# Second layer of a hybrid decoder trunk: the state-space mixer's operands turned at the layer boundary instead of in slots 2 to 4

## What is computed

```python
bb_re = f_re[..., None] * br - f_im[..., None] * bi
bb_im = f_re[..., None] * bi + f_im[..., None] * br
x_re = jnp.einsum('bsgi,gpi->bsgp', ug, bb_re)
x_im = jnp.einsum('bsgi,gpi->bsgp', ug, bb_im)
...                                   # h_t = a h_(t-1) + x_t, complex
y = (jnp.einsum('gip,bsgp->bsgi', c_re, h_re)
     - jnp.einsum('gip,bsgp->bsgi', c_im, h_im) + d_skip * ug)
```

## Time and profile before

| | |
|---|---|
| median of 3 runs | 969.76 us (968.94 to 971.78) |
| the profiled execution | 969.32 us, its span 967.6 us |
| PE busy | 937.2 us, 97% of the span |
| PEld busy | 785.7 us, 81% |
| DVE, ACT, POOL busy | 700.1, 591.8, 282.9 us |
| mean granted TensorE clock | 0.996 |
| DMA | 157.32 MB, 163 GB/s on average |

### The profile page before, as it was taken

How to read it: one execution, slowest core, us unless ns; L and a number is a source line. 1 busy time by engine, 2 the same in 40 slices (tenths; PEclk the granted TensorE clock), 3 DMA queues, 4 the chain that set the end, 5 groups by cost and what they waited for, 6 DMA issues and landing times. The chain is left out here.

```text
span 967.6 us, 16077 instructions
## 1 busy us (share of the span) xinstructions
PE 937.2 (97%) x5895; PEld 785.7 (81%) x5895; DVE 700.1 (72%) x1127; ACT 591.8 (61%) x955; POOL 282.9 (29%) x226
## 2 busy tenths in 40 slices
PE   8989999999999999999999999999999999999996
PEld 7879777777878888888889987777777788888885
DVE  6878967664666888798865668766557668777776
ACT  7426776768355765666654567767664566666654
POOL 0243334341420568466000224443206001011010
PEclk9989999999999999999999999999999999999999
DMA  7963433453554756556469543434535346655551
GB/s 215 269 195 106 134 129 131 131 159 103 174 174 137 199 189 201 175 194 195 135 164 272 153 131 112 135 118 117 174 131 174 131 152 199 213 174 195 194 175 44
DMA packets 138023, 157.32 MB, mean 163 GB/s; under 512 B 16641, under 2 KB 105321, under 8 KB 137962
## 3 DMA queue, kind: packets, MB, share of 16 engines
q1 hardware_dynamic: 137960, 156.51, 52.2%
q10 hardware_dynamic: 2, 0.00, 0.0%
HBM read 154.40 MB, written 1.05 MB: 161 GB/s over the span
## 5 line engine op out<-in xcount | busy, mean ns | idle before, releaser
L1672 DVE TENSOR_TENSOR wl<-ring,wh 128x1024 fp32r<-128x1024 f32 (+1 forms) x276 | 359.8, 1306 | 100.1 <-ACT wh L1357 98.9
L1357 ACT ACTIVATE wh<-ring 128x1024 fp32r<-128x1024 f32 (+1 forms) x276 | 287.9, 1045 | 153.1 <-PE pj L791 120.5
L791 PE MATMUL pj<-h,wh 128*128 128x512 f32 (+1 forms) x1344 | 297.0, 344 | 11.9 <-DVE wl L1672 10.0
L791 PE MATMUL pj<-wh,h 128*128 128x512 f32 (+1 forms) x832 | 273.4, 395 | 4.7 <-ACT gate L1344 2.4
L791 PEld LDWEIGHTS pj<-h,wh 128*128 128x128 f32 x1344 | 229.3, 192 | 39.9 <-issue 11.7
L791 PEld LDWEIGHTS pj<-wh,h 128*128 128x128 f32 x832 | 154.7, 188 | 47.4 <-issue 10.4
L791 PE MATMUL pj<-h,wl 128*128 128x256 f32 x1024 | 189.7, 284 | 0.0
L791 PEld LDWEIGHTS pj<-h,wl 128*128 128x128 f32 x1024 | 158.4, 192 | 6.9
L791 PE MATMUL pj<-wl,h 128*128 128x512 f32 (+1 forms) x416 | 159.5, 383 | 0.0
L2322 POOL TENSOR_TENSOR work<-work 128x512 f32<-128x512 f32 x20 | 40.8, 2040 | 266.7 <-DVE work L2120 199.7
L791 PEld LDWEIGHTS pj<-wl,h 128*128 128x128 f32 x416 | 78.4, 188 | 12.8
(11 more groups left out here) (304 smaller groups left out, 1241.5 us busy)
## 6 DMA issues: line engine op xcount, KB each, us to landing
ring<-in_ffn_w_up SPq DMA_DIRECT2D x44, 1024.0 KB, 5.1
ring<-in_w_in SPq DMA_DIRECT2D x40, 1024.0 KB, 5.1
ring<-in_ffn_w_down SPq DMA_DIRECT2D x22, 1024.0 KB, 4.9
ring<-in_w_in SPq DMA_DIRECT2D x16, 512.0 KB, 5.5
ring<-in_w_branch SPq DMA_DIRECT2D x8, 1024.0 KB, 5.1
ring<-in_w_out SPq DMA_DIRECT2D x8, 1024.0 KB, 5.1
ring<-in_w_branch SPq DMA_DIRECT2D x8, 512.0 KB, 6.0
ring<-in_w_in SPq DMA_DIRECT2D x8, 256.0 KB, 3.9
```

The costliest lines, as they stand in the source:

```text
L791: return nc.tensor.matmul(o, a, b, start=start, stop=stop, skip_group_check=True)
L1357: A(dst, src, ACT.Copy).then_inc(w_hi.sem, 1)
L1672: TT(dst, src, hi.bitcast(F32), ALU.subtract).then_inc(w_lo.sem, 1)
```

## The change

In the second layer alone (`l == 1`) the S5 operands are turned at the layer boundary; the first layer stays as it was.

- `s5_c` (eight turns) stands where the `idle(6, bO)` at the end of the first layer's MLP was. It uses `bO` and `bY` and first waits for `unit_out[1]` too. The last layer keeps its idle products.
- `s5_b(0)` (eight turns, into `bO` and `bY`) stands behind the turning of token tile 0, in place of the `idle(4)` there.
- `s5_direct` (64 instructions, into `bX[0]`) and `s5_b(1)` (eight turns) stand behind the turning of token tile 1, in place of the `idle(4)` there.
- ACT copies the turned operands out (`operands_out`, two copies each time) behind the split of piece 0, behind the squares of token tile 1 and behind the split of piece 4.
- DVE's `s5_diagonal` stands behind the split of piece 4.
- POOL's `s5_carried` keeps its place in POOL's queue, and waits in addition for `hq_done`, since it writes where the first compression weights lie.

```diff
             for l in range(DEPTH):
                 turn_normed(2 * l, 0)
+                if l:
+                    s5_b(l, 0, (bO, bY))
                 if l == 0:
                     pe.wait_ge(step_row.sem, 2)
                     nc.tensor.transpose(bO[:, 0:P], stP, ident).then_inc(lam_turned.sem, 1)
                     idle(4)
                     turn_normed(2 * l, 1)
-                idle(4)
+                    idle(4)
...
                 if l:
                     turn_normed(2 * l, 1)
-                    idle(4)
+                    s5_direct(l, bX[0])
+                    s5_b(l, 1, (bO, bY))
...
-                    if q == S5_C:
-                        s5_c()
-                    if q in S5_B:
-                        s5_b(S5_B.index(q))
-                    if q == S5_B[0]:
-                        s5_direct()
+                    if l == 0 and q == S5_C:
+                        s5_c(l, (bY, bX[0]))
+                    if l == 0 and q in S5_B:
+                        s5_b(l, S5_B.index(q), bX)
+                    if l == 0 and q == S5_B[0]:
+                        s5_direct(l, bY)
...
-                idle(6, bO)
+                if l + 1 < DEPTH:
+                    pe.wait_ge(unit_out[1].sem, unit_out[1].at(l, n // 2 + 1))
+                    s5_c(l + 1, (bO, bY))
+                else:
+                    idle(6, bO)
                 pe.wait_ge(a_split.sem, a_split.at(l, STEPS))
...
+            def operands_out(l, step, banks):
+
+                for h in range(2):
+                    n = 2 * step + h
+                    a.wait_ge(bc_turned.sem, bc_turned.at(l, n + 1))
+                    dst = (CL[:, 0], CL[:, 1], BL[:, 0:4], BL[:, 4:8], BL_im[:, 0:4], BL_im[:, 4:8])[n]
+                    A(dst, banks[h].rearrange("p (j q) -> p j q", j=JC), ACT.Copy).then_inc(bc_ready.sem, bc_ready.up())
...
                 if l:
                     split_hi(l, 0)
+                    operands_out(l, 0, (bO, bY))
                 square(n, 0, 0)
...
                 square(n, 1, 1)
+                if l:
+                    operands_out(l, 1, (bO, bY))
                 root(n, 1)
...
                 split_hi(l, 4)
+                if l:
+                    operands_out(l, 2, (bO, bY))
...
-                    if q in (S5_C, *S5_B):
-                        n = 2 * (q - S5_C)
-                        for n in (n, n + 1):
-                            a.wait_ge(bc_turned.sem, bc_turned.at(l, n + 1))
...
+                    if l == 0 and q in (S5_C, *S5_B):
+                        operands_out(l, q - S5_C, (bY, bX[0]) if q == S5_C else bX)
...
                 for s in range(3, 5):
                     split_lo(l, s)
+                if l:
+                    s5_diagonal(l, bX[0])
...
-                    if q == S5_B[1]:
-                        s5_diagonal()
+                    if l == 0 and q == S5_B[1]:
+                        s5_diagonal(l, bY)
...
                 def s5_carried():
 
+                    g.wait_ge(hq_done.sem, hq_done.at(l, 1))
                     g.wait_ge(bc_ready.sem, bc_ready.at(l, 2))
```

More of the change, by code:

```diff
@@ L865, in idle, with s5_c, s5_b, s5_direct @@
                     mm(o[:, 0:P], ident, ident, True, True)
+            def s5_c(l, banks):
+                for c in range(2):
+                    pe.wait_ge(cx_ready.sem, cx_ready.at(l, c + 1))
+                    for j in range(JC):
+                        ins = nc.tensor.transpose(banks[c][:, P * j:P * j + P], cx[:, c, j, :], ident)
+                    ins.then_inc(bc_turned.sem, bc_turned.up())
+            def s5_b(l, c, banks):
+                if c == 0:
+                    pe.wait_ge(bx_ready.sem, bx_ready.at(l, 2))
+                pe.wait_ge(bc_ready.sem, bc_ready.at(l, 2 + 2 * c))
+                for h in range(2):
+                    for j in range(4):
+                        s = 8 * h + 2 * j
+                        ins = nc.tensor.transpose(banks[h][:, P * j:P * j + P],
+                                                  bx[:, c, s:s + 2].rearrange("p t n i -> p (t n i)"), ident)
+                    ins.then_inc(bc_turned.sem, bc_turned.up())
+            def s5_direct(l, o):
+                pe.wait_ge(bc_ready.sem, bc_ready.at(l, 2))
+                for j in range(JC):
+                    for c in range(2):
+                        for e in range(4):
+                            r = 32 * e
+                            ins = nc.tensor.matmul(o[r:r + 32, P * j:P * j + P], bx[:, c, 4 * j + e, 0, :],
+                                                   CL[:, c, j, :], start=c == 0, stop=c == 1, skip_group_check=True,
+                                                   tile_position=(0, r))
+                ins.then_inc(k_done.sem, k_done.up())
             pe.wait_ge(ones_set.sem, 1)
@@ L1012, in cmp_turn @@
                     ins.then_inc(pc_done.sem, pc_done.up())
[L1014 to L1043, removed]
                 def nsa_scores(m):
@@ L1785, in turns, with s5_diagonal @@
                 v.wait_ge(turns_ready.sem, 1)
+            def s5_diagonal(l, o):
+                v.wait_ge(k_done.sem, k_done.at(l, 1))
+                at = [P, JC, 4, 32]
+                TT(K0.rearrange("p j (e i) -> p j e i", e=4), o.rearrange("p (j e i) -> p j e i", j=JC, e=4),
+                   kon[:, K_QUAD:K_QUAD + 4].rearrange("p (j e i) -> p j e i", j=1, i=1).broadcast_to(at), ALU.mult)\
+                    .then_inc(k_ready.sem, k_ready.up())
             def table(tmp, lo, hi, first, last):
@@ L2005, in s5_scan @@
                     ins.then_inc(g5_ready.sem, g5_ready.up())
[L2007 to L2013, removed]
                 if l:
```

## The result

| | before | after |
|---|---|---|
| median of 6 runs each, us | 970.07 (968.7 to 971.78) | 964.98 (963.45 to 966.09) |
| ratio | | 0.9947, 95% interval 0.9935 to 0.996 |
| profiled execution: time, span, us | 969.32, 967.6 | 965.8, 964.1 |

What follows compares the result with a forecast made beforehand. TensorE was taken to bound the kernel, in slots 1 to 5 but for one gap. -4.54 - 1.3 - 0.45 + 1.95 + 0.3 = -4.04 gave 965.3 from the profiled execution, 965.7 by the median; forecast 965.5, range 964.0 to 967.6.

Steps and rivals of the forecast that it cites:

- blocks out of slots 2 to 4, and the gap: Second layer: S5 blocks leaving slots 2 to 4, gain 4.54 us; split wait at slot 6 gone, gain 1.3.
- first layer's end: Ahead of the last down-projection: eight turns replace twelve idle instructions, gain 0.45 us, bounds 0 and 0.67.
- down-projection and tile 0: Token tile 0, TensorE: eight turns replace eight idle instructions, 1.03 against 1.06 us; nothing.
- tile 1: Token tile 1, TensorE: `s5_direct` and `s5_b(1)` replace idle products, 2.95 for 1.00, delaying `vg`; loss 1.95 us, bounds 1.7 and 2.2.
- ACT ahead of the `vg` copy-out: Behind piece 4's split: two ACT copies delay the `vg` copy-out and first `narrow`; loss 0.3 us, bounds 0 and 0.5.
- behind slot 6: From slot 6 on: the same work, 4 us earlier.
- Rival 4: Slots: weight supply sets their pace, the 5.8 us return as split waits; 971.1 us, chance 0.05.
- rival 2: Slot 6: the split wait stays or returns one or two slots on; gain 2.7 us, chance 0.12.
- Tile 0, ACT: ACT copies behind the squares, 1.08 us, fit its 1.24 wait ahead of the root; nothing, up to 0.2 without that cover.
- POOL: `s5_carried` starts about 10 us earlier; slowing a DVE split would meet 6.8 us of DVE waiting; nothing.
- Rival 5: Layer boundary: turning lets the clock fall, 2.7 us per fall; 973.3 us with three falls, chance 0.05.
- case 2: The outcome in which the gap at slot 6 stays or moves: 966.6 to 967.0 us, chance 0.12.

Runs made afterwards that it cites:

- e7: The changed kernel again, without an edit; 966.1 us, ratio 0.9966.
- e1: Changed kernel with `s5_direct`, the imaginary part, its copies and mask back in slots 3 and 4, idle products back at tile 1; 968.01 us.
- e2: Kernel before, with ACT's exponential of the compressed softmax ahead of the two `BL_im` copies in slot 4, both layers; 969.3 us.
- e5: Changed kernel plus four idle products (eight instructions) behind the turning of the imaginary part, ahead of `vg` of tile 1; 966.07 us.
- e9: Changed kernel with `s5_direct` in two halves (first at tile 0) and, in the first layer, DVE's slot 6 split ahead of the softmax; 962.23 us, ratio 0.9926.
- e8: Changed kernel, `s5_direct` halved (first at tile 0); first layer: ACT's exponential ahead of `BL_im` copies, DVE's slot 6 split ahead of softmax; 963.12 us, ratio 0.9934.
- e6: Changed kernel with the first half of `s5_direct` moved between the first and second `vg` groups of tile 0; 963.19 us.
- e3: Changed kernel with 56 more turns ahead of `s5_c` at the first layer's end; 973.01 us.

## Why the prediction was right, step by step

Predicted was 965.5 (964.0 to 967.6), measured 964.98 at first and 966.1 the second time (e7). The mechanism was right at each step, and the sizes by the marks are:

| step | predicted, us | measured, us | from |
|---|---|---|---|
| blocks out of slots 2 to 4, and the gap | -5.84 | -5.97 | N to S6, 68.04 to 62.07 |
| of it `s5_c` and `s5_b(0)` | | -1.86 | e1 |
| first layer's end | -0.45 | -0.51 | 0.85 in place of 1.36 |
| down-projection and tile 0 | 0 | -0.03 | 7.04 (483.79 to 490.83) against 7.07; from there to the second half of tile 1's turns 5.45 in both |
| tile 1 | +1.95 | +1.83 | 2.74 and 0.09 of switching, less 1.00 |
| ACT ahead of the `vg` copy-out | +0.3 | +0.02 | V to N |
| behind slot 6 | 0 | +0.13 | S6 to end |
| sum | -4.04 | -4.53 | |

**Slots and gap.** Both terms came as counted, and e1 and e2 separate them: the first two blocks alone give their length and leave the gap, ACT's order alone gives the gap and leaves the blocks. Rival 4, that weight supply sets the pace there, falls with e1. The gap didn't move either (rival 2). The timeline of ACT shows that the softmax had more room than I gave it:

```profile
558.79 1.28 ACT L1570 ACT_TABLE_LOAD   x1
560.73 0.41 ACT L1570 ACTIVATE cE<-work 128x240 f32<-128x240 f32 x1 [0.66 <-DVE work L1965]
```

And that of DVE:

```profile
560.29 0.41 DVE L1965 TENSOR_TENSOR work<-work,hid 128x240 f32<-128x240 f32 x1
...
562.65 2.36 DVE L1687 TENSOR_TENSOR wl<-ring,wh 128x1024 fp32r<-128x1024 f32 x2
```

Even in its bound, the prediction had the table load start when DVE's first half is done. It starts at 558.79, before that half has even begun (559.14), and ends ahead of the exponential's wait. The split for slot 6 ends at about 563.83 (562.65 and half of 2.36) and is wanted at 566.05. That is 2.2 us to spare, not 1.2: the table load, 1.28 us, was counted in a chain in which it doesn't stand. The term was at its bound already, so this changed no number, only the chance of rival 2, which was too high.

**Tile 1.** The block is as long as `s5_direct` and `s5_b(1)` were in their slots, and it stands whole on the path (e5). Taking slot durations for it was right to 0.12, and the 0.12 is a misreading. I split the 2.91 of `s5_b(0)` with `s5_direct` into 0.91 and 2.0; the trace before has `s5_direct` start at 558.51, which gives 1.03 and 1.88.

**ACT behind it.** This is the term that was mis-sized, 0.3 for 0.02. The timeline of ACT, against the earlier trace rows:

```profile
500.74 1.84 ACT L1365 ACTIVATE wh<-ring 128x560 fp32r<-128x560 f32 x2 [3.16 <-PE pj L791]
502.48 1.07 ACT L1384 ACTIVATE gate<-pj 128x512 f32<-128x512 f32 x2
503.43 0.39 ACT L1434 ACTIVATE vn<-pj 128x256 f32<-128x256 f32 x1
```

I subtracted the idle 0.74 from the 1.08 of the copies. But starts count: the copies held ACT from 502.48 to 503.43, 0.95, since one operation's end overlaps the next one's start. The copy-out starts 3.83 after V (503.43 - 499.60), against 3.69 before (500.97 - 497.28), so it is 0.14 late. And `narrow` doesn't hang on it. TensorE's last `vg` product before `narrow`, in the kernel before and after:

```profile
501.42 0.29 PE L791 MATMUL pj<-wh,h 128*128 128x280 f32 x1
```

```profile
503.75 0.29 PE L791 MATMUL pj<-wh,h 128*128 128x280 f32 x1
```

`narrow` starts 0.22 us behind this product before (501.64) and 0.23 after (503.98), with no wait in brackets. So TensorE's own queue of `vg` products set its start, not ACT's copy-out, and ACT's 0.14 didn't reach it. The cover is nearly used up, though: the copy-out's second piece ends at 503.89, 0.09 ahead of `narrow`, where it ended 0.21 ahead before (501.43). V to N is 4.37 or 4.38 in every kernel with the block and 4.38 in e1 without it.

**Tile 0, ACT.** ACT's wait ahead of the root shrank from 1.24 to 0.27 us, since the copies stand in it, as the prediction had it by a narrow margin.

**POOL.** `s5_carried` moved up and does slow DVE beside it. From the timelines of POOL and of DVE:

```profile
546.10 2.97 POOL L2284 TENSOR_TENSOR s5h<-CL,s5p 128x1024 f32<-128x1024 f32 x1 [8.03 <-PE bA L1006]
549.03 1.92 POOL L2285 TENSOR_TENSOR mr<-CL,s5p 128x1024 f32<-128x1024 f32 x1
```

```profile
547.21 1.91 DVE L1944 TENSOR_SCALAR ng<-ng 128x48 f32<-128x48 f32 x1
...
549.64 2.39 DVE L1687 TENSOR_TENSOR wl<-ring,wh 128x1024 fp32r<-128x1024 f32 x1
```

The scalar operation, 0.18 us before, takes 1.91, and a split, 1.23 us alone, takes 2.39. Before, too, a split beside `s5_carried` took 2.10 (from 554.82). Nobody on TensorE waited for either, since DVE had 6.8 us of waiting to lose here. "Nothing" was right because the cover was large, not because the contention was small.

**The size against the runs.** By the marks the steps came to 0.49 more than predicted: 0.28 at the ACT term, 0.13 in the slots, 0.12 at tile 1, 0.06 at the layer's end and 0.03 at tile 0, less 0.13 behind slot 6. This is less than half of what one kernel's median moved between two measurements (1.1 us). So that 965.5 and 964.98 lie so close is in part luck: the same sum, held against the second measurement, is off the other way.

**Two slips in the prediction's own sums.** Rival 5 "decides from two falls on (970.7)", but by its own 0.3% anything below 972.7 is no change, so it takes three. And the 967.0 of case 2 holds the runs' offset of 0.44 already; with an unhidden copy (0.2) it ends at 967.2, not at 967.6. Neither touches the forecast.

## What to carry to other kernels

Work that replaces filler is not free because filler stood there: find out whether the filler covers a wait (then only its excess is paid) or stands on the path, and look for a wait next to it that can take half of the new work, as at tile 0 here. When an instruction waits long for one thing and others queue behind it, put the one that is ready first in front, and try such reorderings one at a time: in the first layer, up to slot 6, ACT's new order saved 0.62 us (e2), DVE's 1.40 (e9), and both together 0.14 (e8). Below half a per cent, compare two traces by intervals between marks around the change, not by their spans: here the intervals repeat to 0.04 us, while the spans of the changed kernel's first six runs reach from 961.7 to 964.4.

## What the runs showed of the hardware that was not expected

**The spread has a place.** It lies in the first 75 us, in three pieces. From the first compression products to W it is 411.03 us before, 411.10 after and 411.19 in e7. The first piece is the start: TensorE's first product waits for a small DMA, 2.31 us in the profiled execution before and 3.43 after:

```profile
3.43 3.75 PE L791 MATMUL pj<-gate,kr 1*128 1x512 f32 x4 [3.43 <-DMA gate<-in_norm_mix]
```

The second is the way from there to the end of a wait of TensorE of 3 to 4 us near 60 us: 57.39 us after (3.43 to 60.82), but 58.05 in e7 (2.31 to 60.36) and 56.68 in e6 (3.19 to 59.87). The third is the stretch of half clock behind that wait. In the execution after, by stretch:

```profile
60.00:62.00 2.00, 1.18 (x5) 1.21 (x6) 2.00 (x3) 0.00 (x0) 0.00 (x0) 0.50 0.00 0
...
64.00:66.00 2.00, 2.00 (x11) 2.00 (x11) 1.56 (x3) 0.00 (x0) 0.00 (x0) 0.53 1.07 378
```

And in e6, whose code up to there is the same:

```profile
60.00:62.00 2.00, 2.00 (x14) 2.00 (x15) 1.97 (x3) 0.00 (x0) 0.00 (x0) 0.74 0.01 3
...
64.00:66.00 2.00, 2.00 (x18) 2.00 (x17) 1.01 (x2) 1.06 (x1) 0.00 (x0) 0.90 0.77 272
```

In e6 the clock fell later and came back earlier. From the end of the wait to the first compression products it took 10.28 us there (59.87 to 70.15), 11.02 after (60.82 to 71.84), 11.31 in e7 (60.36 to 71.67). The longest is 11.50, in e3. What makes these pieces differ from one execution to the next is open; it wasn't tried.

**Turning keeps the clock.** 64 turns of 128 x 128 in 32 bits one behind the other (6.97 us in e3) left the granted clock at 1.00, and a turn takes 0.110 us from start to start (6.17 / 56), an ordinary product of that size 0.113 (6.35 / 56).

**A table load does not wait for its activation's input.** It starts when ACT's queue reaches it: at 558.79 for an activation that starts at 560.73, and in e8 at 87.12 for one at 93.84.

**What small tiles cost at their edge.** The 64 small products of `s5_direct` take 1.89 us from start to start (496.86 to 498.75), and the turns ahead of them need 0.09 us more than with idle products behind them (0.58 against 0.49); it is 0.58 in e7 and 0.59 in e6 too, and 0.49 in e1, which has idle products there.
